# Moving the split weights' buffers by 192 bytes inside the on-chip memory of a two-block transformer kernel

## The chip, the cores and the metric

The kernel runs on one core of a Trainium2 chip. The metric is the device time of one execution, in microseconds (us); lower is better. Before the change three executions took 967.9, 968.3 and 972.03 us, median 968.3 us.

## What is computed

The reference runs two transformer blocks, one after the other, on 256 tokens of width 1024, all in 32-bit floats. Cut to its weight products, which are what the kernel spends its time on:

```python
# block 1
px = modulate(rms_norm(x, g_pre_mix), sh_m, sc_m) @ w_in        # 1024 x 2320, also for 256 context tokens
att_x = window_attention(...); ml_x = mlstm(...)                # two mixers
x = x + gt_m * rms_norm(concat(att_x, ml_x) @ w_out, g_post_mix)
x = x + gt_f * rms_norm(swiglu(modulate(rms_norm(x), ...), w_ffn_in, w_ffn_out), g_post_ffn)   # 1024 -> 2 x 2816 -> 1024
# block 2, on 16 + 256 tokens
h = h + 0.5 * swiglu_2(rmsnorm(h, ffn1_norm), w_gate, w_up, w_down)
ya, yb = window_sink_attention(...), gated_linear_attention(...)   # from rmsnorm(h) @ w_in, 1024 x 4368
h = h + (sigmoid(gate_a) * (ya @ w_branch_att) + sigmoid(gate_b) * (yb @ w_branch_gla)) @ w_out
h = h + 0.5 * swiglu_2(rmsnorm(h, ffn2_norm), w_gate, w_up, w_down)
return rmsnorm(h, final_norm)[16:]
```

## The kernel before

**The split.** Each 32-bit weight `w` is used as a pair `hi` and `lo` in the tensor engine's faster 32-bit format (`F32R`): `hi = round(w)`, `lo = w - hi`. The activations are pairs too (`n_high`/`n_low`, `g_high`/`g_low`, `mixH`/`mixL`, `n5H`/`n5L`). A product is three matmuls that add into one accumulator: high by high, low activation by `hi`, high activation by `lo` (`split_mm`, lines 2005 to 2007). The weight tile (128 x 128) is the stationary operand, loaded by a weight load of its own (LDWEIGHTS, shown as PEld); the activations (256, 258 or 272 tokens wide) are the moving operand. The exceptions are `by_token` (lines 2203 to 2205), where the activations are stationary and the weights move, 512 wide, and `keep_clock` (line 2484), where one tile of `hi` is stationary and 512 columns of `hi` move.

**The ring.** SyncE issues the DMAs of the weights into `raw` (four slots of 1408 columns, 5632 bytes each). ScalarE copies a slot to `hi` (line 621), VectorE subtracts it into `lo` (line 1143), TensorE uses the pair. The slot is free for the next DMA when `lo` is made; `hi` and `lo` are free when TensorE has done the slot's matmuls (`mm_done`). The four slots go round through all phases in this order: `win0`, `winq`, `winm`, `winv`, `wino` (products of `w_in` beside block 1's attention and mLSTM), `wout`, `gu0` and `dn0` (block 1's gate and up, then down products of the feed-forward), `gu1` and `dn1` (block 2's first feed-forward), `in2k` and `in2g` (products of block 2's `w_in`), `brb`, `bra`, `wout2`, `gu2` and `dn2`. Each engine's order is written out by hand; there is no scheduler.

**Where the tables lie.** The tensors are allocated one after the other in the order of the `sbuf(...)` lines, each at a multiple of 32 bytes in every one of the 128 partitions. A tensor allocated in a stack that is closed again (`slabs1`, `staged`) gives its place back to what follows, so `slab_hi` (four slabs of `w_ada`, used at the very start) lies where `hi` lies, and `stage` where `mixH` lies. From these sizes come the starts; what matters for the prediction is the rest of each start when divided by 256:

| tensor | start, byte of the partition | rest by 256 | step from one 128-row tile of it to the next |
|---|---|---|---|
| `raw` | 33184 | 160 | slots 22 x 256 |
| `hi`, `slab_hi` | 55712 | 160 | slots 22 x 256, tiles of 512 bytes |
| `lo` | 78240 | 160 | as `hi` |
| `sinkn`, `negm` | 100768, 100832 | 160, 224 | |
| `mixH`, `mixL` | 100960, 109152 | 96, 96 | 1024: rest stays 96 |
| `n5H`, `n5L` | 144928, 161312 | 32, 32 | 2048: rest stays 32 |
| `n_high`, `n_low` as `nH`, `nL` (258 or 272 wide) | 121888, 132128 | 32, 32 | 1088: rest goes 32, 96, 160, 224 and round |
| the same as `mH`, `mL` (272 wide) | | 32 | 1280: rest stays 32 |
| the same without the 16 leading tokens (256 wide) | | 96 | 1280: rest stays 96 |
| `g_high`, `g_low` in `dn0`, `dn2` (256 wide) | 168032, 192096 | 96, 96 | 1024: rest stays 96 |
| `g_high`, `g_low` in `dn1` (272 wide) | | 96 | 1088: rest goes round |

Every moving and every stationary operand named here starts 32 bytes past a multiple of 64.

Of the kernel before, what the change touches and what calls it, by code (L numbers as in the profile page):

```python
# [14 lines left out]
P = 128  # L15
# [99 lines left out]
def program(nc, dr, out):  # L115
    with ExitStack() as root:
        def sbuf(stack, name, shape, dt=F32):
            return stack.enter_context(nc.sbuf_tensor(name, shape, dt))
# [12 lines left out]
        crow = sbuf(root, "crow", [P, D])  # L131
        R = sbuf(root, "R", [P, KD, TM])
        raw = sbuf(root, "raw", [P, RING, SLOT])
        slabs1 = ExitStack()
        slab_hi = sbuf(slabs1, "slab_hi", [P, RING, SLOT])
        slabs1.close()
        hi = sbuf(root, "hi", [P, RING, SLOT], F32R)
        lo = sbuf(root, "lo", [P, RING, SLOT], F32R)
        sinkn = sbuf(root, "sinkn", [P, 16])
        negm = sbuf(root, "negm", [P, 32])  # L140
        staged = ExitStack()
        stage = sbuf(staged, "stage", [P, 4, 1024])
        staged.close()
# [2655 lines left out]
```

## Time and profile before

| what | value |
|---|---|
| median of three executions | 968.3 us |
| the profiled execution's span, first to last instruction | 969.3 us |
| TensorE, matmuls busy | 954.7 us (98%), 7543 of them |
| TensorE, weight loads busy | 886.8 us (91%) |
| VectorE busy | 640.4 us (66%) |
| ScalarE busy | 494.7 us (51%) |
| share of TensorE in the chain that ended last | 88% |
| granted TensorE clock, mean | 0.999 of full |
| moved by DMA | 176.06 MB, mean 182 GB/s |

The profile's own time of the profiled execution is its span; it is 1.0 us over the median. A matmul's record runs from its start until its result is through, some 280 ns for 256 columns, while the next one starts after some 115 ns: matmuls overlap, so the rate has to be read from how many start in a stretch, not from "mean ns of one".

### The profile page before, as it was taken

To read this page: it belongs to the slowest core of one execution; us is meant where nothing else is said; L and a number is where in the kernel's file an instruction comes from. 1 tells how busy PE (TensorE), PEld (TensorE's weight loads), DVE (VectorE), ACT (ScalarE), POOL (GpSimd) and SP (SyncE) were. 2 spreads that over 40 slices of the span, in tenths; PEclk is the share of its full clock that TensorE was granted. 3 is DMA by queue.
4 is the path that set the end of the run, shared out by engine and by line. 5 is a ranking of instruction groups with operands and counts; after the bars stand their busy time and mean duration, and the time that the engine had idled before them with its cause. 6 is when DMAs were issued, how large, how long until landed. Compare 5 with 4: busy or idle time off the path is not lost.

```text
span 969.3 us, 19405 instructions
## 1 busy us (share of the span) xinstructions
PE 954.7 (98%) x7543; PEld 886.8 (91%) x7543; DVE 640.4 (66%) x990; ACT 494.7 (51%) x762; POOL 68.8 (7%) x100
## 2 busy tenths in 40 slices
PE   8999999999999999999999999999999999999997
PEld 3776778899999999899999999999989999999997
DVE  4788887687666774765555546665778666565654
ACT  3755547664454543554444434645565555444540
POOL 0012002200000021000000000200210100000000
PEclk9999999999999999999999999999999999999999
DMA  9982437546566795276665944663445567567841
GB/s 348 384 282 89 131 131 237 181 165 201 180 187 184 203 299 164 63 215 174 173 174 169 238 114 137 212 185 88 132 134 173 167 181 209 179 182 220 215 119 43
DMA packets 189184, 176.06 MB, mean 182 GB/s; under 512 B 7313, under 2 KB 177825, under 8 KB 188753
## 3 DMA queue, kind: packets, MB, share of 16 engines
q1 hardware_dynamic: 183456, 154.29, 53.7%
q0 software_dynamic: 4960, 17.64, 5.2%
q10 hardware_dynamic: 720, 3.49, 0.9%
q8 instruction: 31, 0.51, 0.2%
q14 instruction: 17, 0.13, 0.1%
HBM read 174.32 MB, written 1.05 MB: 181 GB/s over the span
## 4 chain that ended last, share of the span: by engine, by line
PE 88%; DVE 6%; DMA 2%; ACT 2%; issue 1%; SPq 1%; POOL 0%; DVEq 0%; ACTq 0%
PE acc L2005 24%; PE acc L2006 24%; PE acc L2007 24%; PE acc L2398 2%; DMA slab_hi<-in_w_ada 1%; DMA stage<-in_w_late 1%; PE acc L2203 1%; PE acc L2205 1%; PE acc L2204 1%; PE wk L2005 1%; DVE lo L1143 1%; PE wk L2007 1%; PE wk L2006 1%; PE wk L2702 1%; PE wk L2134 1%
## 5 line engine op out<-in xcount | busy, mean ns | idle before, releaser
L1143 DVE TENSOR_TENSOR lo<-raw,hi 128x1024 fp32r<-128x1024 f32 (+1 forms) x259 | 331.6, 1291 | 211.4 <-ACT hi L621 211.1
L621 ACT ACTIVATE hi<-raw 128x1024 fp32r<-128x1024 f32 (+1 forms) x260 | 283.6, 1099 | 133.7 <-PE acc L2007 123.5
L2005 PE MATMUL acc<-n_high,hi 128*128 128x272 f32 (+3 forms) x1016 | 290.8, 286 | 0.3 <-DVE hbuf L1671 0.3
L2006 PE MATMUL acc<-n_low,hi 128*128 128x272 f32 (+3 forms) x1016 | 289.4, 285 | 0.0
L2007 PE MATMUL acc<-n_high,lo 128*128 128x272 f32 (+3 forms) x1016 | 288.4, 284 | 0.0
L2005 PEld LDWEIGHTS acc<-n_high,hi 128*128 128x128 f32 (+1 forms) x1016 | 191.6, 189 | 2.7 <-issue 1.4
L2006 PEld LDWEIGHTS acc<-n_low,hi 128*128 128x128 f32 (+1 forms) x1016 | 191.1, 188 | 0.5
L2007 PEld LDWEIGHTS acc<-n_high,lo 128*128 128x128 f32 (+1 forms) x1016 | 191.0, 188 | 0.2
L2006 PE MATMUL acc<-g_low,hi 128*128 128x256 f32 (+1 forms) x528 | 149.1, 282 | 0.0
L2005 PE MATMUL acc<-g_high,hi 128*128 128x256 f32 (+1 forms) x528 | 148.9, 282 | 0.0
L2007 PE MATMUL acc<-g_high,lo 128*128 128x256 f32 (+1 forms) x528 | 148.7, 282 | 0.0
L2005 PE MATMUL acc<-mixH,hi 128*128 128x256 f32 x400 | 113.0, 282 | 0.5 <-DVE gab L1844 0.4
L2006 PE MATMUL acc<-mixL,hi 128*128 128x256 f32 x400 | 112.3, 281 | 0.0
L2007 PE MATMUL acc<-mixH,lo 128*128 128x256 f32 x400 | 112.3, 281 | 0.0
L2006 PEld LDWEIGHTS acc<-g_low,hi 128*128 128x128 f32 x528 | 99.8, 189 | 0.0
L2005 PEld LDWEIGHTS acc<-g_high,hi 128*128 128x128 f32 x528 | 99.2, 188 | 0.2 <-issue 0.2
L2007 PEld LDWEIGHTS acc<-g_high,lo 128*128 128x128 f32 x528 | 99.2, 188 | 0.0
L2006 PEld LDWEIGHTS acc<-mixL,hi 128*128 128x128 f32 x400 | 76.6, 192 | 0.0
L2005 PEld LDWEIGHTS acc<-mixH,hi 128*128 128x128 f32 x400 | 75.1, 188 | 1.4 <-DVE gab L1844 0.7
L2007 PEld LDWEIGHTS acc<-mixH,lo 128*128 128x128 f32 x400 | 75.1, 188 | 0.0
L566 POOL TENSOR_TENSOR sq<-sq 128x256 f32<-128x256 f32 (+1 forms) x28 | 25.6, 915 | 479.9 <-ACT sq L923 431.9
L923 ACT ACTIVATE sq<-R (+3 forms) x36 | 15.9, 440 | 57.6 <-DVE R L1715 49.9
(424 smaller groups left out, 1246.6 us busy)
## 6 DMA issues: line engine op xcount, KB each, us to landing
raw<-in_w_in SPq DMA_DIRECT2D x52, 512.0 KB, 4.1
raw<-in_w_ffn_in SPq DMA_DIRECT2D x44, 512.0 KB, 3.8
raw<-in_ffn_w_gate SPq DMA_DIRECT2D x44, 512.0 KB, 3.9
raw<-in_ffn_w_up SPq DMA_DIRECT2D x44, 512.0 KB, 3.8
raw<-in_ffn_w_down SPq DMA_DIRECT2D x32, 704.0 KB, 4.8
stage<-in_w_late POOLq DMA_DIRECT2D x24, 512.0 KB, 5.1
raw<-in_w_ffn_out SPq DMA_DIRECT2D x16, 704.0 KB, 6.2
raw<-in_w_out SPq DMA_DIRECT2D x16, 512.0 KB, 4.4
```

Source lines behind the costliest of these rows:

```text
L566: ins = pool.tensor_tensor(sq[:, 0, 0:width], sq[:, 0, 0:width], sq[:, k, 0:width], ALU.add)
L621: act.activation(hi[:, j, 0:width], raw[:, j, 0:width], ACT.Copy).then_inc(hi_ready, 1)
L923: act.activation(sq[:, k, 0:width], R[:, k, t0:t0 + width], ACT.Square).then_inc(sq_ready, 1)
L1143: dve.tensor_tensor(lo[:, j, 0:width], raw[:, j, 0:width], hi[:, j, 0:width].bitcast(F32), ALU.subtract).then_inc(lo_ready, 1)
L2005: pe.matmul(out_, wH, xH, start=start, stop=False)
L2006: pe.matmul(out_, wH, xL, start=False, stop=False)
L2007: return pe.matmul(out_, wL, xH, start=False, stop=stop)
L2134: ins = pe.matmul(bank[:, T * m:T * m + T], ws[:, j, w], xs[:, k, 0:T], start=k == 0 and m == 0 and n == 0, stop=k == KD - 1 and n == 2, s ...
L2203: pe.matmul(out_, n5H[:, k, rows], hi[:, k // 2, w], start=k == 0, stop=False)
L2204: pe.matmul(out_, n5H[:, k, rows], lo[:, k // 2, w], start=False, stop=False)
L2205: return pe.matmul(out_, n5L[:, k, rows], hi[:, k // 2, w], start=False, stop=k == KD - 1)
L2398: ins = pe.matmul(out_, ws[:, j, w], xs[:, k, :], start=k == 0 and m == 0 and n == 0, stop=k == KD - 1 and n == 2, skip_group_check=True)
```

## The change

The two small tables `sinkn` (64 bytes) and `negm` (128 bytes) are allocated ahead of `slab_hi`, `hi` and `lo` instead of behind them. `hi`, `slab_hi` and `lo` so start 192 bytes later (55904 and 78432; rest by 256: 96 in place of 160), and the two tables lie right behind `raw` (55712 and 55776; rests 160 and 224, as before). All that is allocated behind them, `stage` and `mixH` first, stays where it was, as does `raw`. No instruction, wait, DMA or size is added, removed or reordered.

```diff
         raw = sbuf(root, "raw", [P, RING, SLOT])
+        sinkn = sbuf(root, "sinkn", [P, 16])
+        negm = sbuf(root, "negm", [P, 32])
         slabs1 = ExitStack()
         slab_hi = sbuf(slabs1, "slab_hi", [P, RING, SLOT])
         slabs1.close()
         hi = sbuf(root, "hi", [P, RING, SLOT], F32R)
         lo = sbuf(root, "lo", [P, RING, SLOT], F32R)
-        sinkn = sbuf(root, "sinkn", [P, 16])
-        negm = sbuf(root, "negm", [P, 32])
```

## Rows read from the trace of the kernel before

**Rows 1.** Page, busy time and share of each engine.
```profile
PE 954.7 (98%) x7543; PEld 886.8 (91%) x7543; DVE 640.4 (66%) x990; ACT 494.7 (51%) x762; POOL 68.8 (7%) x100
```
**Rows 2.** Page, chain that ended last, shares.
```profile
PE 88%; DVE 6%; DMA 2%; ACT 2%; issue 1%; SPq 1%; POOL 0%; DVEq 0%; ACTq 0%
```
**Rows 3.** Stretches, TensorE: us from:to, length, busy us (matmuls seen), clock, DMA.
```profile
179.20:189.80 10.60, 10.60 (x96) 1.00 0.55 160
332.00:386.00 54.00, 54.00 (x479) 1.00 0.81 231
...
699.50:701.90 2.40, 2.40 (x23) 1.00 0.64 194
...
738.20:753.20 15.00, 15.00 (x130) 1.00 0.69 210
754.00:781.00 27.00, 27.00 (x229) 1.00 0.59 175
782.00:897.00 115.00, 115.00 (x979) 1.00 0.67 194
902.00:958.00 56.00, 56.00 (x477) 1.00 0.53 142
```
**Rows 4.** Groups by form, TensorE, of 340 to 380 and of 910 to 950.
```profile
L2005 PE MATMUL acc<-g_high,hi 128*128 128x256 f32 x118 | 32.6, 276 | 0.0
...
L2005 PE MATMUL acc<-g_high,hi 128*128 128x256 f32 x114 | 32.0, 281 | 0.0
```
**Rows 5.** Stretches, TensorE, of other widths and starts.
```profile
200.00:326.00 126.00, 126.00 (x1040) 1.00 0.59 177
415.00:528.00 113.00, 113.00 (x906) 1.00 0.66 190
530.00:594.00 64.00, 64.00 (x511) 1.00 0.58 158
600.00:610.00 10.00, 10.00 (x81) 1.00 0.84 262
```
**Rows 6.** Instructions in time, TensorE, `gu0`: each sixth matmul (start us, us).
```profile
234.03 0.28 PE L2005 MATMUL acc<-n_high,hi 128*128 128x258 f32 x1
...
234.76 0.29 PE L2005 MATMUL acc<-n_high,hi 128*128 128x258 f32 x1
...
235.50 0.28 PE L2005 MATMUL acc<-n_high,hi 128*128 128x258 f32 x1
...
236.22 0.28 PE L2005 MATMUL acc<-n_high,hi 128*128 128x258 f32 x1
...
236.93 0.28 PE L2005 MATMUL acc<-n_high,hi 128*128 128x258 f32 x1
```
**Rows 7.** In time, TensorE, `in2k`: 16-column weight tiles, then 128-column ones.
```profile
597.51 0.28 PE L2006 MATMUL acc<-n_low,hi 128*16 128x272 f32 x1
...
598.75 0.29 PE L2007 MATMUL acc<-n_high,lo 128*16 128x272 f32 x1
598.87 0.29 PE L2005 MATMUL acc<-n_high,hi 128*128 128x272 f32 x1
...
606.10 0.29 PE L2005 MATMUL acc<-n_high,hi 128*128 128x272 f32 x1
```
**Rows 8.** Chain of waits in time, merged: start us, us, what.
```profile
6.03 11.50 DMA slab_hi<-in_w_ada
...
31.22 2.84 PE wk L2134 x24
```
**Rows 9.** Page, DMA issues at the start: count, KB each, median us to landing.
```profile
slab_hi<-in_w_ada SPq DMA_DIRECT2D x4, 512.0 KB, 11.3
stage<-in_w_ada SPq DMA_DIRECT2D x4, 512.0 KB, 10.8
slab_n<-in_w_ada SPq DMA_DIRECT2D x4, 512.0 KB, 12.0
```
**Rows 10.** Groups by form, VectorE and ScalarE: count, busy us, mean ns, idle before.
```profile
L1143 DVE TENSOR_TENSOR lo<-raw,hi 128x1024 fp32r<-128x1024 f32 x207 | 252.3, 1229 | 153.8 <-ACT hi L621 153.5
L1143 DVE TENSOR_TENSOR lo<-raw,hi 128x1408 fp32r<-128x1408 f32 x48 | 78.0, 1635 | 57.0 <-ACT hi L621 57.0
L1607 DVE TENSOR_TENSOR R<-R,Y 128x256 f32<-128x256 f32 x16 | 6.8, 424 | 0.5
L621 ACT ACTIVATE hi<-raw 128x1024 fp32r<-128x1024 f32 x208 | 217.1, 1051 | 88.3 <-PE acc L2007 85.5 <-DMA raw<-in_w_in 2.5
```

## The prediction, made before the changed kernel was run

> **What bounds the kernel now.** I read the busy shares first, then the chain of waits, then the rate of TensorE's matmuls stretch by stretch. TensorE has matmuls in flight 98% of the span, VectorE is busy 66%, ScalarE 51% [rows 1]; 88% of the chain that ended last is TensorE [rows 2], and the clock was granted in full in every stretch looked at [rows 3, 5], which is the 2.4 GHz level. So the kernel's time is the number of wide matmuls (about 5,800 of the 7,543) times the time from one start to the next, and a change of one nanosecond in that time is worth some 5.8 us. Nothing else can be moved by a change that removes no work.
>
> The time from start to start is the stretch's length over its matmuls, less the two that were already in flight when the stretch began. For 256 columns it has two values. From 332 to 386 us it is 54 / 477 = 113.2 ns, near 180 us 10.6 / 94 = 112.8; from 782 to 897 it is 115 / 977 = 117.7 ns and from 902 to 958 56 / 475 = 117.9 [rows 3]. The two levels show also in a matmul's own record, 276 against 281 ns [rows 4]. The remarkable thing is that `dn0` (332 to 386) and `dn2` (902 to 958) are the same code with the same tensors at the same bytes: the level is not decided by the operands' places alone, but is something that a stretch falls into and stays in. In the pieces between 630 and 738 us, where small matmuls of attention stand between pieces of 24, most are at the low level (at 699.5 us 2.4 / 21 = 114 ns), and from 738 us to the end all are at the high one: 15 / 128 = 117.2 ns and 27 / 227 = 118.9, with a short wait in it, come before the two already named [rows 3].
>
> **The change part by part.** It removes, adds and moves no instruction. What moves is three sets of bytes.
>
> (1) *`hi` and `lo` as stationary operands, rest by 256 from 160 to 96.* First the question whether places matter to TensorE at all. They do for the moving operand. In `gu0` the moving tile starts at rests 32, 96, 160, 224 in turn, and six matmuls take 0.73, 0.74, 0.72 and 0.71 us in turn [rows 6], so the time of one matmul depends on where the moving tile starts. So something in TensorE's reading has a period of 256 bytes, and 192 is not a multiple of that. The shift can act through the stationary operand only if the weight load's reading and the moving stream get in each other's way. The nearest row on that: with the same moving tiles, weight tiles of 16 columns go at (598.75 - 597.51) / 10 = 124.0 ns and those of 128 columns at (606.10 - 598.87) / 57 = 126.8 ns [rows 7]. An eighth of the weight bytes makes 2.8 ns of difference, while the time over the 113.3 ns that 272 columns need at 2.4 GHz is 10.7 ns even with the small tiles. Most of the loss over the ideal belongs to the moving stream by itself, whose place doesn't change in the main phases.
>
> By this row the effect of the stationary operand's place lies between -2.8 ns a matmul (all the contention gone) and +2.8 ns (it doubles). Where the moving rest goes round all four values (`gu0`, `gu1`, `dn1`: 121.4, 125.0 and 125.7 ns by the first three of [rows 5]) a shift of the weights by 64 bytes only turns the cycle, and the mean stays: 0. Where the moving rest is fixed, about 3,240 matmuls of 256 columns, it could act: bounds -9 and +9 us. I take 0, since the row nearest to it says that the weights' reading is the small part, and the two levels at equal places say that something else picks the level. The phases with moving rest 32 (`in2k` at 272 columns, 10 / 79 = 126.6 ns [rows 5]; the 256-column products at the start, 2.84 / 24 = 118.3 ns [rows 8]) are some 330 matmuls; if they went to the best value of their width they would give back about 1 us.
>
> The Trainium skill speaks against any effect: SBUF — State Buffer, section "Who interferes with whom", gives TensorE two read ports of its own, one for the moving operand and one for the weight load, and says that it never waits on anyone. The 2.8 ns between small and large weight tiles [rows 7] don't agree with full independence, though they don't show a conflict by address either. By that page the sum is 0 exactly, by the row it is 0 with 9 us on either side.
>
> (2) *`hi` and `lo` as moving operands*, in `by_token` (144 matmuls by the code, 512 wide) and `keep_clock` (some 26): they go from rest 160 to 96. In `gu0` six matmuls differ by at most 0.03 us between rests [rows 6], 5 ns each; at twice the columns perhaps 10 ns, so 170 x 10 ns: bounds -1.7 and +1.7 us; I take 0.
>
> (3) *ScalarE writing `hi` from `raw`, VectorE writing `lo` from `raw` and `hi`.* So far all three lie at equal rests, afterwards `raw` is at 160 and the others at 96. VectorE's 1024- and 1408-column forms give (1635 - 1229) / 384 = 1.057 ns a column and 147 ns fixed [rows 10]. `R<-R,Y`, whose inputs lie at different rests, should by that take 147 + 256 x 1.057 = 418 ns, and takes 424 [rows 10]. Equal or unequal rests cost the same within 6 ns; 256 x 6 ns = 1.5 us on an engine that idles a third of the span and waits for ScalarE more than it makes TensorE wait (154 us of idle before these instructions). On the path: 0. ScalarE waits 85.5 us for TensorE before its copies [rows 10], which covers it likewise. If the cover were gone, 1.5 us would be the price.
>
> (4) *The first slabs of `w_ada`, DMA into `slab_hi`.* This DMA is on the path: the chain waits 11.50 us for it [rows 8]. Its destination goes from rest 160 to 96, where `stage` lies, whose slabs land in 10.8 us against 11.3; `slab_n`'s at rest 32 need 12.0 [rows 9]. Bounds -0.5 and +0.7 us, taken 0. `sinkn` and `negm` keep their rests.
>
> The sum is 969.3 + 0, which stands 1.0 us over the median of the three executions, so 968.3 us.
>
> **The rivals.**
>
> *The low level all through (faster).* What picks a stretch's level must be something that carries on from the work before. If it is the relation of the two reading streams, the shift deals it anew. From 738 to 960 us some 1,880 matmuls stand at 117.8 ns; at 113.3 they would take 1,880 x 4.5 ns = 8.5 us less: 959.8 us. For it: most of the short pieces before 738 us already fall to the low level [rows 3], and this stretch holds the larger part of what can flip. Against it: four stretches in a row, parted by short waits, stayed high [rows 3], so whatever decides it is stable, and the moving operands, whose places do matter, stay put.
>
> *The low level lost (slower).* The same mechanism the other way: `wout`, `dn0` and the 256-column pieces of `in2k` and `in2g` hold about 190 + 530 + 640 = 1,360 matmuls at the low level. At 117.8 ns they cost 1,360 x 4.5 ns = 6.1 us: 974.4 us. It decides as soon as moving and stationary operand at equal rests (96 and 96, as after the change) make the start of the two streams meet, which they now do a quarter of the period apart. For it: the low level is the narrower state, 113.3 ns being found at no width but 256 and at no rest but 96. Against it: [rows 7] again.
>
> *A third level.* Contention at rests 96 on 96 that is new, or gone, over all 3,240 matmuls, by up to the 2.8 ns of [rows 7]: 959.3 or 977.4 us.
>
> *The change doesn't do what it says*: the tables might be rounded up differently and the shift be another one. Both are multiples of 32 bytes, so I give it nothing.
>
> **How the numbers follow.** No effect: 0.38. Low level all through: 0.28. Low level lost: 0.22. A third level: 0.12, half on each side. Faster by over 0.5% (which is about what a measurement of this kernel can tell from no change, 4.8 us): 0.28 + 0.06 = 0.34. Slower by over 0.5%: 0.22 + 0.06 = 0.28. Within: 0.38. The likeliest case is 968.3 us, and by itself it would range from 966 to 971, the small terms of (2) and (4). Cases of both signs hold more than half, so the range reaches to both rivals: from the third level's low end, 959.3, over 974.4 to 976.0.
>
> **What would show it.** Right: in the profile after, 56 us from 902 on hold 477 matmuls and 54 us of `dn0` hold 479, records of 281 and 276 ns; `gu0` and `gu1` unchanged. The faster rival: some 497 in 56 us of `dn2` and records of 276 ns in `gu2`. The slower one: `dn0` at 281 ns and a later start of `gu1`. Any change of `gu0`'s or `gu1`'s rate would prove the turning of the cycle wrong, and with it (1). VectorE's 1229 and ScalarE's 1051 ns should stay within 10 ns; if they don't and the time moves while TensorE's rates stay, (3) was wrong. The forecast fails if the level is set by how the two streams lie to each other.

## The result and the profile after

Four executions of the changed kernel took 981.9 to 984.0 us, median 982.8; the kernel before, with one more execution beside them, 969.6 (four, 967.9 to 972.0). The ratio is 1.0128, with a 95% interval of 1.0103 to 1.0152: the change costs 1.3%, some 13 us. The forecast was 968.3 us with a range up to 976.0; the result lies above the range. The profiled execution took 982.65 us with a span of 980.9, so the time is 1.75 us over the span.

First the page of the changed kernel: busy times, then the shares of the chain, as in [rows 1, 2].

```profile
PE 966.9 (99%) x7543; PEld 898.7 (92%) x7543; DVE 640.4 (65%) x990; ACT 494.6 (50%) x762; POOL 67.8 (7%) x100
...
PE 88%; DVE 6%; DMA 2%; ACT 2%; issue 1%; SPq 1%; POOL 0%; DVEq 0%; ACTq 0%
```

The same instructions, the same 88% of TensorE in the chain, VectorE and ScalarE busy as long as before to 0.1 us; matmuls are busy for 12.2 us more (954.7 to 966.9) and weight loads for 11.9 more. All of the loss is in TensorE. Where, the stretches show (columns as in rows 3: from:to, length, busy us with the matmuls seen, clock, DMA share, GB/s), placed in the same phases as [rows 3, 5]: `gu0`, `dn0`, `gu1`, `dn1`, `in2k` at 272 columns, branches and `wout2`, `gu2`, `dn2`.

```profile
200.00:326.00 126.00, 126.00 (x1038) 1.00 0.59 178
333.00:387.00 54.00, 54.00 (x452) 1.00 0.79 222
415.00:528.00 113.00, 112.71 (x902) 1.00 0.65 188
535.00:597.00 62.00, 62.00 (x494) 1.00 0.60 163
603.00:613.00 10.00, 10.00 (x83) 1.00 0.67 208
741.00:756.00 15.00, 15.00 (x130) 1.00 0.57 179
785.00:900.00 115.00, 115.00 (x956) 1.00 0.64 186
910.00:966.00 56.00, 56.00 (x469) 1.00 0.52 142
```

`dn0` is the plainest: 54 us held 479 matmuls, now 452, 54 / 450 = 120.0 ns where it was 113.2. `dn2`, at the high level before (477 in 56 us), is slower too: 469, 119.9 ns; `gu2` 956 where 979 were. So neither of the two old levels is there any more in the main phases: all stretches of 256 columns whose moving operand lies at rest 96 go at 120.0 ns. `gu0` (1038 beside 1040) and `gu1` (902 beside 906, with 0.29 us of idle time in it) kept their rates. The clock stands at 1.00, the 2.4 GHz level, in each of them.

The records themselves, by form, from 341 to 381 us and from 915 to 955:

```profile
L2005 PE MATMUL acc<-g_high,hi 128*128 128x256 f32 x112 | 31.7, 283 | 0.0
...
L2005 PE MATMUL acc<-g_high,hi 128*128 128x256 f32 x112 | 31.7, 283 | 0.0
```

276 and 281 ns in [rows 4], 283 ns in both now. `dn0` and `dn2`, so far different with the same code and bytes, are alike.

From the starts of all matmuls in the two traces (mean of the time from one start to the next inside unbroken work) the account by phase is this; "relation" is the start of the moving operand less that of the stationary one, taken by 256 (so -128 and +128 are the same). "All four in turn" stands where the moving start goes round.

| phase | matmuls | relation before, after | ns before | ns after | us of the phase, before, after |
|---|---|---|---|---|---|
| 256-column products at the start (`n5H`) | 144 | -128, -64 | 118.6 | 115.5 | 19.2, 18.8 |
| `by_token`, 512 columns | 144 | -128, +64 (the weights move: 160 less 32, then 96 less 32) | 232.5 | 229.8 | 35.8, 35.6 |
| `wout` | 192 | -64, 0 | 114.3 | 119.7 | 22.9, 24.3 |
| `gu0`, 258 columns | 1056 | all four in turn | 120.8 | 120.8 | 127.9, 127.9 |
| `dn0` | 528 | -64, 0 | 113.4 | 120.0 | 60.1, 63.4 |
| `gu1`, 272 columns | 1056 | all four in turn | 125.1 | 125.1 | 134.1, 134.1 |
| `dn1`, 272 columns | 528 | all four in turn | 125.9 | 126.1 | 66.5, 66.6 |
| `in2k`, 272 columns, large tiles | 192 | -128, -64 | 126.6 | 123.4 | 24.6, 23.8 |
| `in2k` and `in2g`, 256 columns | 624 | -64, 0 | 114.3 | 119.7 | 74.6, 77.7 |
| `brb`, `bra` | 192 | -64, 0 | 116.4 | 119.8 | 23.0, 23.6 |
| `wout2` | 192 | -64, 0 | 117.8 | 120.0 | 22.7, 23.0 |
| `gu2` | 1056 | -64, 0 | 117.8 | 120.0 | 124.6, 126.9 |
| `dn2` | 528 | -64, 0 | 117.8 | 120.0 | 62.3, 63.4 |

The rows from -64 to 0 lose 12.1 us, those from -128 to -64 give 1.2 us back and `by_token` 0.2. That is 10.7 of the 11.6 us between the spans (980.9 and 969.3); the rest is in the phases' ends. The 115.5 ns of the first row is a mean of stretches at two levels, 113.8 ns (from 51.6 us) and up to 117.8 ns (from 29.3 us): the old pair, now where the relation is -64.

The places where I looked for small terms. The chain of the changed kernel in time (start us, us, what), its wait for the first slabs and the products of [rows 8]:

```profile
5.98 11.42 DMA slab_hi<-in_w_ada
...
31.08 2.83 PE wk L2134 x24
```

And VectorE's and ScalarE's groups by form, as in [rows 10]:

```profile
L1143 DVE TENSOR_TENSOR lo<-raw,hi 128x1024 fp32r<-128x1024 f32 x207 | 252.4, 1229 | 159.1 <-ACT hi L621 158.9
L1143 DVE TENSOR_TENSOR lo<-raw,hi 128x1408 fp32r<-128x1408 f32 x48 | 77.5, 1624 | 60.7 <-ACT hi L621 60.7
...
L621 ACT ACTIVATE hi<-raw 128x1024 fp32r<-128x1024 f32 x208 | 217.1, 1051 | 92.8 <-PE acc L2007 89.7 <-DMA raw<-in_w_in 2.9
```

1229 and 1051 ns as before, with `raw` and `hi` now at different rests; only the idle time before them grew (the copies wait 89.7 us for TensorE where they waited 85.5).

### The profile page after: what moved, and what is told of

It reads as the page before. It is cut to its first block, busy times and chain, and to the rows that moved or that the text cites. A ratio compares the mean times of both kernels' runs of the same rounds, so it can differ in the third digit from the quotient of the medians.

```text
span 980.9 us, 19405 instructions
## 1 busy us (share of the span) xinstructions
PE 966.9 (99%) x7543; PEld 898.7 (92%) x7543; DVE 640.4 (65%) x990; ACT 494.6 (50%) x762; POOL 67.8 (7%) x100
## 4 chain that ended last, share of the span: by engine, by line
PE 88%; DVE 6%; DMA 2%; ACT 2%; issue 1%; SPq 1%; POOL 0%; DVEq 0%; ACTq 0%
PE acc L2005 24%; PE acc L2006 24%; PE acc L2007 24%; PE acc L2398 3%; DMA slab_hi<-in_w_ada 1%; DMA stage<-in_w_late 1%; PE acc L2203 1%; PE acc L2205 1%; PE acc L2204 1%; PE wk L2005 1%; DVE lo L1143 1%; PE wk L2007 1%; PE wk L2006 1%; PE wk L2702 1%; PE wk L2134 1%
## 5 line engine op out<-in xcount | busy, mean ns | idle before, releaser
L621 ACT ACTIVATE hi<-raw 128x1024 fp32r<-128x1024 f32 (+1 forms) x260 | 283.6, 1098 | 141.5 <-PE acc L2007 134.1
L2005 PE MATMUL acc<-mixH,hi 128*128 128x256 f32 x400 | 113.8, 285 | 0.4 <-DVE gab L1844 0.4
L2006 PE MATMUL acc<-mixL,hi 128*128 128x256 f32 x400 | 113.2, 283 | 0.0
L2007 PE MATMUL acc<-mixH,lo 128*128 128x256 f32 x400 | 113.2, 283 | 0.0
```

Source lines behind the costliest of these rows:

```text
L621: act.activation(hi[:, j, 0:width], raw[:, j, 0:width], ACT.Copy).then_inc(hi_ready, 1)
L2005: pe.matmul(out_, wH, xH, start=start, stop=False)
L2006: pe.matmul(out_, wH, xL, start=False, stop=False)
L2007: return pe.matmul(out_, wL, xH, start=False, stop=stop)
```

## The experiments

Theory R says: what counts is the relation of the two starts, moving less stationary. Rivals are that `hi`'s and `lo`'s own place counts, that the distance is felt in pieces of 64 bytes only, and, for the two levels, that they belong to what runs beside. Each group of experiments ran beside the kernel before on the same chip; ratios are to that. The rates in ns are from each run's one profiled execution: where a stretch's count over its length is given, the two matmuls already in flight are taken off; other rates are means from start to start in unbroken work. The first four shared one chip, where the kernel before took 971.0 us.

**One table alone in front, both ways.** `e1_sinkn_first` leaves `negm` behind:

```diff
+        sinkn = sbuf(root, "sinkn", [P, 16])
         slabs1 = ExitStack()
...
         lo = sbuf(root, "lo", [P, RING, SLOT], F32R)
-        sinkn = sbuf(root, "sinkn", [P, 16])
         negm = sbuf(root, "negm", [P, 32])
```

> Only the 64-byte table stands in front, so hi and lo move by 64 bytes in place of 192 (rest by 256: 224). Theory R (what counts is the moving operand's start minus the stationary one's, by 256): moving 96 on 224 is the relation -128, which the 256-column products on n5H had in the kernel before (32 on 160) at 118.3 ns. So all 3,240 matmuls of 256 columns go at about 118.3 ns: 1,360 x 5.0 + 1,880 x 0.5 = 7.7 us more than before, about 977 us; gu0 and gu1 unchanged at 120.8 and 125.0 ns. Rival P (the place of hi by itself counts, 160 being a good one and others bad): 120.0 ns as after the change, about 982 us, in gu0 and gu1 something changes too.

Measured: 981.0 us, ratio 1.0106 (1.0089 to 1.0122). At relation -128 the stretches go at 118.7 ns (`dn0`, `wout`, `gu2`), `dn2` at 119.9 (120.0 once settled). The time alone is nearer to the rival's 982 us than to R's 977; R's sum left out the 1.75 us between span and time, took 118.3 for 118.7 ns (1.1 us) and had `dn2` at that level too (0.8 us). It is the rates, and the next runs, that part the two. `e2_negm_first` moves `negm` (128 bytes) and leaves `sinkn` behind, so that the relation is +64:

> Only the 128-byte table stands in front: hi and lo move by 128 bytes (rest 32), moving 96 on 32 is the relation +64, which no main phase has had yet. Theory R: in gu0 (258 columns) the moving rest goes through all four relations at a mean of 120.8 ns, some 120.0 for 256 columns; with 120.0 at relation 0, 118.3 at -128 and 113.3 to 117.8 at -64 the fourth would be 480 - 120.0 - 118.3 - 115.5 = some 126 ns: 3,240 x (126 - 116) = 32 us more than before, about 1001 us. Rival P: no worse than after the change, 120.0 ns and 982 us. Both: gu0, gu1 as before if only relations count.

Measured: 973.3 us, ratio 1.0026 (1.0016 to 1.0036). R's estimate of 1001 us was wrong, and so was the rival's 982: +64 behaves like -64, with the same two levels 113.3 and 117.8 ns (`dn0` 113.7, `wout2` 114.2, `dn2` 117.8). Stretches of the two, `dn0`, `gu2` and `dn2` by time, first `e1_sinkn_first`:

```profile
333.00:387.00 54.00, 54.00 (x458) 1.00 0.78 224
785.00:895.00 110.00, 110.00 (x924) 1.00 0.64 187
910.00:960.00 50.00, 50.00 (x419) 1.00 0.58 159
```

and `e2_negm_first`:

```profile
333.00:387.00 54.00, 54.00 (x479) 1.00 0.81 231
785.00:895.00 110.00, 110.00 (x936) 1.00 0.66 193
910.00:960.00 50.00, 50.00 (x427) 1.00 0.48 126
```

In the last row 50 / 417 = 119.9 against 50 / 425 = 117.6 ns. A shift of the same tensors by 128 bytes costs 2.5 us, one of 64 costs 10 us.

**Relation or own place?** `e3_after_no_pad_n` is the changed kernel without the 64 unused bytes ahead of `n_high`, so that `n_high`, `n_low`, `g_high` and `g_low` come 64 bytes earlier while `hi`, `lo` and `mixH`, `mixL` stay:

```diff
         ffn = ExitStack()
-        sbuf(ffn, "pad_n", [P, 16])
         n_high = sbuf(ffn, "n_high", [P, KD * 320], F32R)
```

> The changed kernel with the 64-byte filler ahead of n_high left out, so that n_high, n_low, g_high and g_low move down by 64 bytes as well (256-column starts at rest 32 on hi at 96), while mixH, mixL stay at 96. Theory R: the relation of dn0, dn2, and the 256-column pieces of in2k, in2g and wout2 is -64 again, so they return to 113.3 or 117.8 ns, and gu2, brb, bra and wout (mixH) stay at 120.0: 973 us if the levels are those of the kernel before, 970 if dn2 is low too. Rival A (the moving operand's own rest 96, or the stationary's rest 160, makes the good level): all stay at 118 ns or more, 981 us or above.

Measured: 975.8 us, ratio 1.005 (1.003 to 1.0071).

```profile
333.00:387.00 54.00, 53.99 (x476) 1.00 0.81 229
785.00:895.00 110.00, 110.00 (x919) 1.00 0.65 189
910.00:960.00 50.00, 50.00 (x427) 1.00 0.55 145
```

`dn0` is back at 54 / 474 = 113.9 and `dn2` at 117.6 ns with `hi` and `lo` where the change put them; `gu2`, whose moving operand is `mixH`, stays at 110 / 917 = 120.0. That is the cleanest of the runs: within one kernel the phases with relation -64 have the old levels and those with relation 0 have 120.0 ns. The time lies over R's numbers and under the rival's, so it is the stretches that decide.

The phases whose moving start goes round say the same, tile by tile. Each 128-row tile of `gu0` and `gu1` has six matmuls at one moving start, so their time, divided by six, can be set against the relation (medians over the phase's steady part, ns a matmul):

| kernels | rest of `hi` | relation | `gu0`, 258 columns | `gu1`, 272 columns |
|---|---|---|---|---|
| before, e4, after, e3, e1, e2 | 160, 192, 96, 96, 224, 32 | -128 | 120.8 to 121.0 | 125.8 |
| | | -64 | 123.5 | 123.7 |
| | | 0 | 120.0 | 125.3 |
| | | +64 | 118.8 to 119.0 | 125.2 |
| e5, e6, e10, e11 | 160, 160, 224, 96 | -96 | 120.2 to 120.3 | 125.2 |
| | | -32 | 120.8 to 121.0 | 125.3 to 126.0 |
| | | +32 | 119.3 to 119.5 | 124.2 to 124.7 |
| | | +96 | 122.7 | 125.8 to 126.0 |

With `hi` at five different rests the same relation has the same number, so it is neither `hi`'s nor the moving operand's own place. The values aren't those of a fixed relation: in `gu0` -64 is even the dearest of the cycle. So the sum in the expectation of `e2_negm_first`, which took the mean of the cycle for the mean of four fixed relations, had no ground.

`e4_all_32_later` moves everything by 32 bytes, with 32 unused bytes ahead of `cst` in the kernel before:

```diff
+        sbuf(root, "pad_0", [P, 8])
         cst = sbuf(root, "cst", [P, 3 * P + 2])
```

> The kernel before with a filler of 32 bytes ahead of the first tensor: every tensor, moving and stationary, starts 32 bytes later, all relations by 256 stay. Theory R alone (only the relation counts): nothing changes, 969 us, 113.3 and 117.8 ns. Theory L (the moving operand is fetched in pieces of 64 bytes, 6.67 ns each at 16 columns; a start 32 bytes past a multiple of 64 costs one piece more): 256 columns take 16 pieces in place of 17, 272 columns 17 in place of 18, 258 columns 17 either way. So 256 columns at 107 to 111 ns and 272 at 118 ns, gu0 unchanged: 3,240 x 6.7 + 1,850 x 6.7 = 34 us less, about 935 us.

Measured: 970.8 us, ratio 1.0005 (0.9996 to 1.0015): nothing, so starts at multiples of 64 bytes win nothing and R holds once more. What did change is which stretch has which level: `dn0` was high (117.6 ns) and `dn2` low (113.7), the reverse of before.

```profile
333.00:387.00 54.00, 54.00 (x461) 1.00 0.81 225
910.00:960.00 50.00, 50.00 (x443) 1.00 0.49 129
```

**The map filled in.** Four more relations, each made by unused bytes behind `lo`, which move every moving operand (and the other engines' tensors behind them, so that TensorE's rates in unbroken work decide, not the time). `e5_relation_m32`, the kernel before with

```diff
         lo = sbuf(root, "lo", [P, RING, SLOT], F32R)
+        sbuf(root, "pad_x", [P, 8])
```

> The kernel before with 32 unused bytes behind lo, so that every moving operand lies 32 bytes later and the moving start minus the stationary one is -32 by 256 where it was -64 (and -96 where it was -128). Theory S (the two streams meet in pieces of 64 bytes; a relation in between behaves like one of its two neighbours): the 256-column stretches are either all at the levels of -64, 113.3 or 117.8 ns, and the time is 971 us, or at the 120.0 ns of relation 0, and the time is 983 us. Theory D (the cost goes by the distance of the starts, smoothly): dn2 and gu2 stand between 118 and 120 ns, near 119, and the time is 975 to 978 us. A stretch at a level that is in no run so far (below 113 or above 120.5 ns) would refute both.

Measured: 979.3 us, ratio 1.0083 (1.0057 to 1.011), one single level of 118.3 ns (`dn0` 118.4, `wout2`, `gu2`, `dn2` 118.3). `e6_relation_p32` has `[P, 24]` there:

> The same with 96 bytes: moving start minus stationary start is +32. Relation +64 gave 113.3 or 117.8 ns, relation 0 gave 120.0. Theory S: one of these two, so 971 to 974 us or 983 us, and the same one of them as at -32 if the order of the two starts does not matter. Theory D: between them, 975 to 979 us.

Measured: 973.5 us, ratio 1.003 (1.0011 to 1.005), a level of 116.7 ns (`gu2`, `wout2`, `dn2`; `dn0` 117.7). Theory S is refuted by both, since neither is a level of the neighbours. Theory D isn't borne out either: its times were missed on both sides (979.3 us for 975 to 978, 973.5 for 975 to 979), and -32 and +32, equally far from 0, differ by 1.6 ns. `gu2` and `dn2` of the two, first `e5_relation_m32`:

```profile
785.00:895.00 110.00, 110.00 (x927) 1.00 0.65 187
910.00:960.00 50.00, 50.00 (x425) 1.00 0.59 159
```

then `e6_relation_p32`:

```profile
785.00:895.00 110.00, 110.00 (x944) 1.00 0.68 195
910.00:960.00 50.00, 50.00 (x431) 1.00 0.50 134
```

`e10_relation_m96` is `e1_sinkn_first` with 32 unused bytes behind `lo`:

> The kernel before with sinkn in front (hi, lo 64 bytes later) and 32 unused bytes behind lo: moving start minus stationary start is -96 by 256 for the 256-column phases. A point of the map: so far -128: 118.7, -64: 113.3 or 117.8, -32: 118.3, 0: 120.0, +32: 116.7, +64: 113.3 or 117.8 ns. Theory M (mirror: what counts is the distance from 0 or from 128, and +32 and -32 differ only by the level caught): -96 lies between -64 and -128, 116.7 to 118.7 ns, and the time is 973 to 980 us. A level below 113.3 or above 120.0 ns would refute it.

Measured: 977.3 us, ratio 1.0059 (1.004 to 1.0079); `gu2` and `dn2` 117.3, `wout2` 118.7, `dn0` 120.0 ns, so three levels at one relation, the last outside what I expected. `dn0`, `wout2` and `gu2`:

```profile
333.00:387.00 54.00, 54.00 (x452) 1.00 0.77 221
757.00:777.00 20.00, 20.00 (x171) 1.00 0.58 171
790.00:900.00 110.00, 110.00 (x940) 1.00 0.66 193
```

`e11_relation_p96` is the changed kernel with 96 unused bytes behind `lo`:

> The changed kernel with 96 unused bytes behind lo: relation +96. Theory M: between +64 and +128, 116.7 to 118.7 ns, 973 to 980 us. If instead the rate were set by hi's and lo's own place (rest 96, as in the changed kernel), it would stay at 120.0 ns and 983 us.

Measured: 983.8 us, ratio 1.0128 (1.0075 to 1.018), 120.0 ns in `dn0`, `wout2`, `gu2` and `dn2`. The mirror (+96 as -96) isn't borne out: no stretch at +96 went below 120.0. `gu2`:

```profile
785.00:895.00 110.00, 110.00 (x914) 1.00 0.62 183
```

The second theory of this expectation, that `hi`'s own place at rest 96 costs 120.0 ns wherever the moving one lies, hit this number, but `e3_after_no_pad_n` has `hi` at that place and a mean of 113.4 ns over `dn0`; so it is +96 itself that is bad. For 256 columns this place of `hi` is the only one tried; for 258 columns +96 cost 122.7 ns with `hi` at 96, 160 and 224 alike.

| relation | level seen for 256 columns, ns | runs |
|---|---|---|
| -64 | 113.3 or 117.8 | before, e3 (`dn0`, `dn2`), e4, e7, e8 and those with small matmuls in the kernel before |
| +64 | 113.3 or 117.8 | e2 |
| +32 | 116.7 or 117.8 (`dn0` alone) | e6 |
| -96 | 117.3, 118.7 or 120.0 | e10 |
| -32 | 118.3 | e5 |
| -128 | 118.7 or 120.0 | e1; before, `n5H`: 118.6 |
| 0 | 120.0 | after, e3 (mix phases) |
| +96 | 120.0 | e11 |

**What deals the two levels.** `e8_before_again` is the kernel before, profiled once more:

> The kernel before, unchanged, looked at once more. Theory F (the level that a stretch falls into is a matter of the exact times at its start, so it may differ from one execution to the next): of dn0, wout, wout2, gu2 and dn2 at least one stands at the other of 113.3 and 117.8 ns than in the first look. Theory G (it follows from the program and its places, the same every time): dn0 low and wout2, gu2, dn2 high again, each within 0.3 ns of the first look. Time 968 to 972 us in both.

Measured: 970.5 us. `dn0` 113.4, `gu2` and `dn2` 117.8 ns again, but the stretch from 738 us to a short wait near 753, 117.8 in the first profile, was at 113.3. From 739 to 747 us in the first profile, then in this one:

```profile
739.00:747.00 8.00, 8.00 (x70) 1.00 0.82 241
739.00:747.00 8.00, 8.00 (x73) 1.00 0.79 233
```

So theory G fails for this stretch, while the three long phases repeated as it said; F holds in its words (at least one stretch differs). That alone moves the time by 131 x 4.5 ns = 0.6 us, and a long phase dealt the other way would move it by 2.4 (`dn0`) to 4.7 us (`gu2`), which is of the size of the scatter of the kernel before, 967.6 to 974.3 us in 20 executions.

`e9_nudges` puts small matmuls between the wide ones, of 16 and 64 moving columns in `gu2`'s loop and of 128 and 192 in `dn2`:

```diff
+            def nudge(w, n):
+                pe.matmul(wk[:, 3, 0:n], w, mixH[:, 0, 0:n], start=True, stop=True)
...
                     for s in range(2):
+                        if name == "gu2":
+                            arrived(g + i, 2 * s)
+                            nudge(hi[:, 2 * s, 0:P], 16 if s == 0 else 64)
                         pair(g + i, USE[name] + i, s, *xs, width)
...
                     arrived(BASE[name] + i, j)
+                    if name == "dn2" and j % 2 == 0:
+                        nudge(hi[:, j, 0:P], 128 if s == 0 else 192)
```

> The kernel before with 26 small matmuls added between the wide ones, into a free bank: in gu2's loop one of 16 moving columns ahead of one half of each iteration and one of 64 ahead of the other (18 in all), in dn2 one of 128 and one of 192 columns in each iteration (8). They carry no wait of their own. Theory P (a stretch at relation -64 has two stable ways of running, 113.3 and 117.8 ns, and it takes one by the moment at which its first matmul meets its first weight load): a short matmul in the midst of a stretch is a fresh start, so behind some of the 26 the rate changes between 117.8 and 113.3 ns and then holds to the next; if half fall low, some 790 of the 1,584 matmuls win 4.5 ns, 3.5 us, against 26 short matmuls of some 60 ns, 1.6 us: 967 to 970 us beside 970.5. Theory Q (the level belongs to the phase, to what ScalarE, VectorE and the DMAs do beside it): behind all 26 the rate is 117.8 ns again, and the time is 972 us.

Measured: 973.0 us, ratio 1.0026 (1.0008 to 1.0045). The first of them in time (start us, us, instruction):

```profile
795.74 0.28 PE L2007 MATMUL acc<-mixH,lo 128*128 128x256 f32 x1
795.86 0.17 PE L2451 MATMUL wk<-mixH,hi 128*128 128x16 f32 x1
795.89 0.36 PE L2005 MATMUL acc<-mixH,hi 128*128 128x256 f32 x1
796.09 0.28 PE L2006 MATMUL acc<-mixL,hi 128*128 128x256 f32 x1
```

From 795.74 to 796.09 is 0.35 us where two steps of 117.8 ns would be 0.24: a small matmul costs 0.11 us, not the 0.06 I had put in. One of 64, 128 or 192 columns costs the same (0.10 to 0.12 us). It starts the stretch anew. In the time behind the first of them, and behind the second, here are two starts each that lie 39 matmuls apart:

```profile
796.68 0.28 PE L2005 MATMUL acc<-mixH,hi 128*128 128x256 f32 x1
...
801.10 0.28 PE L2005 MATMUL acc<-mixH,hi 128*128 128x256 f32 x1
...
802.25 0.28 PE L2005 MATMUL acc<-mixH,hi 128*128 128x256 f32 x1
...
806.85 0.28 PE L2005 MATMUL acc<-mixH,hi 128*128 128x256 f32 x1
```

That is 4.42 / 39 = 113.3 and 4.60 / 39 = 117.9 ns. Behind a settling of about five matmuls the first four go at 113.3, 117.8, 117.8 and 113.3 ns (the fourth spends its first five at 114 to 123). Through all 18 of `gu2` the order is one low, two high, six times over, whether the small one had 16 or 64 columns; in `dn2` two of eight are followed by a lasting low level, and a third by one of 33 matmuls that ended at a short wait. In unbroken work at one relation no level changed. The kernel's own short waits deal anew as well: in `e3_after_no_pad_n` `dn2` begins at 113.3 ns and is at 117.8 behind a wait at 906 us. Theory P holds, Q falls; the balance is 26 x 0.11 = 2.9 us against some 380 x 4.5 ns = 1.7 us won.

`e13_after_nudges` puts the same 26 into the changed kernel:

> The changed kernel (relation 0) with the 26 small matmuls of e9. Theory P with one level at relation 0: behind every one the rate comes back to 120.0 ns, the time is 983 + 26 x 0.11 = 985.6 us. If relation 0 too has a lower way of running that the changed kernel only never fell into, a third or so of the 26 stretches stand below 118 ns, and the time is under 983 us; the loss would then be a matter of starts and not of the relation.

Measured: 985.6 us, ratio 1.0151 (1.0116 to 1.0187), as the first case said. Behind the third small matmul, two starts that lie 39 matmuls apart:

```profile
817.09 0.28 PE L2005 MATMUL acc<-mixH,hi 128*128 128x256 f32 x1
...
821.77 0.28 PE L2005 MATMUL acc<-mixH,hi 128*128 128x256 f32 x1
```

That is 4.68 / 39 = 120.0 ns. Behind all 26 the mean comes back to 119.9 or 120.0 ns. So at relation 0 it isn't the luck of the start: 26 fresh starts found no other level.

**The rest that turns.** `e7_nH_fixed_rest` gives `gu0` and `gu1` a fixed relation of -64 in the kernel before:

```diff
-        nH, nL = (n[:, 0:KD * TM].rearrange("p (k t) -> p k t", k=KD) for n in (n_high, n_low))
+        nH, nL = (n[:].rearrange("p (k t) -> p k t", k=KD)[:, :, 16:16 + TM] for n in (n_high, n_low))
```

> The kernel before with one edit: nH and nL are laid with 1280 bytes from tile to tile and 64 bytes in, so the moving operand of gu0 (258 columns) and gu1 (272) starts at rest 96 in every tile, relation -64, instead of going round all four. Theory R (the rate goes by the relation of the two starts, and the mean of a rotation holds its bad values): gu1 falls from 125.06 ns to the 123.4 ns that 272 columns at -64 showed in the changed kernel, 1056 x 1.7 = 1.8 us less; gu0 falls from 120.8 ns to the level of 256 columns and 2 more at 0.42 ns each, 114.2 or 118.6 ns, 1056 x 6.6 or 2.2 = 7.0 or 2.3 us less. Together 4 to 9 us less: 962 to 967 us beside 971 for the kernel before. Theory W (258 and 272 columns are slow by their width, and the rotation has no part in it): both rates stay, 971 us.

Measured: 969.9 us, ratio 0.9994 (0.9975 to 1.0012), so R's 962 to 967 us was missed. `gu0`, then `gu1`:

```profile
202.00:328.00 126.00, 126.00 (x1039) 1.00 0.59 177
417.00:530.00 113.00, 113.00 (x917) 1.00 0.66 190
```

`gu1` went as R said, 113 / 915 = 123.5 ns for 125.1, 1.6 us less. `gu0` did not: 120.8 ns at a fixed relation of -64 as with the turning one. Theory W is right there: 258 columns take at least 3 ns, and at the low level 7.5 ns, more than 256 at the same relation. Between 256 and 512 columns a column costs (232.5 - 118.6) / 256 = 0.44 ns, both at -128, so two more columns explain 0.9 ns of it.

**Dealing the better level.** `e12_two_nudges` is the kernel before with one small matmul ahead of `gu2`'s loop and one in `dn2`'s first iteration:

```diff
+                if name == "gu2":
+                    arrived(g + 2, 0)
+                    nudge(hi[:, 0, 0:P], 16)
                 with pe.Fori(2, COUNT[name]) as i:
...
+                    down_half(name, f, width, 0, 0)
+                    arrived(BASE[name], 2)
+                    nudge(hi[:, 2, 0:P], 16)
+                    down_half(name, f, width, 0, 1)
```

> The kernel before with only two of the small matmuls of e9: one of 16 columns ahead of gu2's loop, and one of 16 columns in the middle of dn2's first iteration. Behind e9's 26 the levels came in a fixed order, one low, two high, and the first in gu2 was low. Theory P (a fresh start deals the level, and the stretch then holds it): gu2 goes at 113.3 ns from about 796 to 898 us, some 860 matmuls x 4.5 = 3.9 us less; dn2's falls low or not, by a third, 460 x 4.5 = 2.0 us. Against 0.11 us for each small one the time is 965 to 967 us beside 970.5. Theory Q (the level belongs to the phase; e9's lows would have come from having many small matmuls): gu2 back at 117.8 ns soon behind the first, 971 us.

Measured: 969.5 us (ten executions, 967.1 to 972.2), ratio 0.9986 (0.997 to 1.0003); the profiled one 968.5. That misses the 965 to 967 us expected and isn't clear of no change, though in the profiled execution `gu2` is at the level hoped for; which levels the other nine had no trace tells. `gu2` ahead of the small matmul and behind it, then `dn2`:

```profile
783.00:796.00 13.00, 13.00 (x112) 1.00 0.49 136
797.00:897.00 100.00, 100.00 (x885) 1.00 0.70 202
...
903.00:955.00 52.00, 52.00 (x444) 1.00 0.49 136
```

13 / 110 = 118.2 ns ahead, 100 / 883 = 113.3 behind, all through 895 matmuls: one fresh start moved the whole rest of `gu2`. `dn2` began low for 32 matmuls, and the second small one threw it to the high level (52 / 442 = 117.6). `e14_nudges_fixed_rest` joins it with `e7_nH_fixed_rest`:

> e12's two small matmuls together with e7's layout of nH and nL (rest 96 in every tile). By the sum of their terms: gu1 123.4 in place of 125.06 ns, 1.8 us less, gu2 low for some 860 matmuls, 3.9 us less, 0.2 us more for the small ones: 965 us, 963 if dn2 falls low. If the other layout moves the moments of the starts (e7's wout2 stretch changed its level by that), gu2 may stay high: 969 us.

Measured: 966.4 us (expected 965), ratio 0.9957 (0.9946 to 0.9967), with `dn2` high again from its small matmul on. `e15_one_nudge` leaves that one out:

> e14 without the small matmul in dn2, which there ended a low stretch of 32 and left 460 matmuls at 117.8 ns. Theory P: with nothing to restart it dn2 stays at 113.3 ns to its end, 460 x 4.5 = 2.1 us and 0.1 us for the small matmul less: 964 us beside e14's 966.4, ratio to the kernel before 0.993. If dn2 turns high by some other start of its own, 966 us.

Measured: 962.9 us, ratio 0.9933 (0.9915 to 0.9951), 6.4 us less than the kernel before beside it and some 20 less than the changed one. `gu1`, `gu2` ahead of and behind the small matmul, `dn2`:

```profile
417.00:530.00 113.00, 113.00 (x918) 1.00 0.65 190
780.50:793.50 13.00, 13.00 (x107) 1.00 0.52 150
795.00:895.00 100.00, 100.00 (x884) 1.00 0.72 206
...
902.00:955.00 53.00, 53.00 (x468) 1.00 0.50 136
```

`dn2` at 53 / 466 = 113.7 ns: left alone it stays low. In this execution `dn0` had been dealt the high level (117.5 ns), and the time of that execution, at 965.2 us, was the longest of its four.

## Why the prediction was wrong

- *The base.* I took the profiled execution as lying 1.0 us over the median. The time is about 1.75 us over the span, in the changed kernel's profiled execution as in `e8_before_again` (970.54 and 968.8), so it was an execution of some 971 us, and 968.3 was the median of only three; twenty others had 970.4. This is 2 us of the 14.5, no part of the ratio.
- *Step (1), the fixed rests: the step that failed.* I put the effect of the stationary operand's place at 0 between bounds of 9 us, on the 2.8 ns between 16-column and 128-column weight tiles [rows 7]. That pair doesn't measure the thing, and it wasn't at one relation either. The wide weight tiles were all at -128, where 272 columns go at 126.6 ns; the 16-column ones lie 64 bytes apart in `hi` (`slice(16 * kk, 16 * kk + 16)`, line 2520), so they went round all four relations. Wide tiles that go round need 125.0 ns (`gu1`, [rows 5]), so of the 2.8 ns some 1.8 were already the effect that I took for nothing, and 1.0 ns is left for the size of the tile. At -64 272 columns go at 123.4, and from -64 to 0 the 256 columns lose 6.7 or 2.2 ns. What the tile's size costs bounds nothing of what the relation costs. The measured term is +12.1 us against the 9 of my bound: a matmul at the low level lost 6.7 ns and one at the high level 2.2, over some 3,300 of them (with my round counts 1,360 x 6.7 + 1,880 x 2.2 = 13.2 us, a little much since not all of the short pieces before 738 us had been low).
- *Step (1), the argument from the two levels.* I read "the same bytes, two levels" as a sign that places don't set the level. What it shows is that a relation can have more than one level and that the start picks; `e9_nudges` shows the picking and `e13_after_nudges` that at another relation there is nothing to pick. Both are true together: the place sets which levels there are, the start which of them.
- *Step (1), the turning.* Right. `gu0`, `gu1` and `dn1` go round all four relations before and after and kept 120.8, 125.1 and 125.9 (126.1) ns. The tile times of `gu0` were 121.0, 123.5, 120.0 and 118.8 ns in turn (the 0.73, 0.74, 0.72 and 0.71 us of [rows 6]) and are 123.5, 120.0, 119.0 and 120.8 now: the same cycle, begun one tile on.
- I had read [rows 6] as "the time of one matmul depends on where the moving tile starts". It depends on where it starts against the weights, as the table by tile shows: that reading was one step away from the answer, since the weights stood still at one rest and only the moving one turned.
- *Step (1), rest 32.* "Would give back about 1 us": measured 1.2, and by the move from -128 to -64.
- *Step (2).* 0 within 1.7 us: `by_token` 232.5 to 229.8 ns, 0.2 us by the phase's length. Right in size; it too went from -128 to +64, while `keep_clock`, whose two operands start at the same byte of `hi`, stayed at 0.
- *Step (3).* Right, 1229 and 1051 ns unchanged. *Step (4).* Right: 11.42 us for 11.50.
- *The rivals.* "The low level lost" named the condition as it is, moving and stationary at equal rests, with a price of 6.1 us and a chance of 0.22. It assumed that 117.8 ns was the floor to fall to. The high level was no floor: it went to 120.0 too, so each low matmul lost 6.7 and not 4.5 ns and each high one 2.2, twice the price. "The low level all through" was the other possible deal; with another kind of change, a fresh start, `e15_one_nudge` had it in `gu2` and `dn2`. "A third level" at rests 96 on 96 is what came, over all the matmuls named, with a chance of 0.06 on the slower side; its price was limited by the same 2.8 ns. The range ended at 976 because its upper ends rested on that 2.8 ns and on 117.8 ns as a floor. The prediction's last line ("fails if the level is set by how the two streams lie to each other") said what came.

The Trainium skill's rule (SBUF — State Buffer, section "Who interferes with whom": two independent read ports of TensorE; "PE and ACT never wait on anyone") gives no effect at all for this change. The runs don't agree: `dn0` takes 113.4 ns a matmul in `e3_after_no_pad_n` and 120.0 in the changed kernel, with the same instructions and the moving operand 64 bytes further. Whether they meet at a port or elsewhere no run here tells.

What stays open: why the levels are what they are; why they come one low, two high behind the small matmuls of `gu2`; whether 256 columns at +96 have a lower level too, since no small matmuls were tried there; whether all executions of a kernel get the same deal, since there is one profile of each and two of the kernel before; and what makes 258 columns so dear.

## What to carry to other kernels

When TensorE's rate is the bound, count matmuls per stretch and compare phases of equal width; if they differ by a few per cent, look at the start of the moving less that of the stationary operand by 256 bytes, before thinking of anything beside them, and try the padding that gives ±64. A table allocated in front of a large buffer moves that relation for every product that reads it, so a change of the allocation order is a change of rate even where no instruction changes. And where one relation has two levels, one cheap fresh start (0.11 us here) at the head of a long phase can deal the better one (0.67% here, with `nH` and `nL` laid anew); it can also deal the worse one, as in `dn2` of `e12_two_nudges`, and only a trace tells.

## What the runs showed of the hardware that I had not expected

- The time from start to start of 256-column matmuls with 128-column weight tiles at full clock is one of a few values: 113.3, 116.7, 117.3, 117.8, 118.3, 118.7, 120.0 ns. The relation of the two starts sets which of them are to be had: 113.3 and 117.8 at ±64, 117.3, 118.7 and 120.0 at -96, only 120.0 at 0 (behind 26 fresh starts). A stretch settles within about five matmuls and then doesn't change for as many as 1,016.
- +64 and -64 are alike for 256 columns. At +96 only 120.0 ns was seen, at -96 three levels from 117.3 to 120.0; for 258 columns going round, +96 is 122.7 and -96 120.3.
- Moving both streams together by 32 bytes does nothing to the time (ratio 1.0005).
- At -64, 272 columns take 123.4 ns but 258 take 120.8: the last 14 columns cost 2.6 ns, and the two before them at least 3.0.
- A small matmul between wide ones costs 0.11 us, with 16 moving columns or with 192.
